# Taps of a depthwise convolution on ScalarE and GpSimd, and a bias product in bfloat16, in a three-layer block

## The reference

```python
def spatial_gating(u_a, v_a, ln_g, ln_b, w_s, b_s):
    u = jax.nn.gelu(u_a, approximate=False)
    v = layer_norm(jax.nn.gelu(v_a, approximate=False), ln_g, ln_b)
    v = v.reshape(bsz, seq // CHUNK, CHUNK, H_A, HD_A)
    w = w_s * jnp.tril(ones)[None]
    mixed = jnp.einsum('hts,bcshd->bcthd', w, v)
    mixed = mixed + jnp.transpose(b_s)[None, None, :, :, None]
    return u * mixed.reshape(bsz, seq, D_A)

def conformer_conv(val_b, gate_b, conv_w, conv_b, ln_g, ln_b):
    g = val_b * jax.nn.sigmoid(gate_b)
    c = depthwise causal convolution of g, 31 taps, + conv_b
    c = layer_norm over each of 4 groups of 128 channels
    return jax.nn.silu(c)
...
mix = jnp.concatenate([a_out, b_out], axis=-1)
x = x + jnp.einsum('bsc,cd->bsd', mix, w_out[l])
h = rms_norm(x, norm2_g[l])
f = jnp.square(jax.nn.relu(h @ w_ff1)); x = x + f @ w_ff2
```

## Time and profile before

| | us |
|---|---|
| median of 3 runs | 2577.37 (2575.87 to 2579.45) |
| profiled execution, its own time | 2576.84 |
| its span | 2575.0 |
| TensorE busy | 2354.4 (91%) |
| VectorE busy | 1537.0 (60%) |
| ScalarE busy | 963.0 (37%) |
| GpSimd busy | 206.9 (8%) |
| mean granted TensorE clock | 0.962 of full speed |

### The profile page before, as it was taken

The page is one execution under the profiler, slowest core; times in us unless marked ns, Lnnn a source line. Parts: engine busy times, 40 slices in busy tenths (PEclk is TensorE's granted clock), DMA queues, the critical chain, the costliest instruction groups (busy, mean ns, idle before and its releaser), DMA issues.

```text
span 2575.0 us, 30098 instructions
## 1 busy us (share of the span) xinstructions
PE 2354.4 (91%) x12784; PEld 1249.0 (49%) x12784; DVE 1537.0 (60%) x1970; ACT 963.0 (37%) x1367; POOL 206.9 (8%) x263
## 2 busy tenths in 40 slices
PE   6999649999999999898999877899999998888899
PEld 4445324444444444344444355664444445666764
DVE  5797766555444555576741388965534406888862
ACT  5244233312121222333221276752322215777741
POOL 0000002000000000432401101012000000000000
PEclk9997869999999999899999999999999998999999
DMA  4010000211111101003100000011130100000021
GB/s 173 33 66 33 33 0 2 97 66 49 50 40 59 66 33 66 33 3 131 66 33 33 33 1 1 1 69 63 66 131 33 67 1 33 1 1 1 1 82 50
DMA packets 50322, 116.00 MB, mean 45 GB/s; under 512 B 2384, under 2 KB 7817, under 8 KB 49804
## 3 DMA queue, kind: packets, MB, share of 16 engines
q1 hardware_dynamic: 48452, 105.39, 11.5%
q10 hardware_dynamic: 1736, 8.68, 0.8%
HBM read 101.49 MB, written 12.58 MB: 44 GB/s over the span
## 4 chain that ended last, share of the span: by engine, by line
PE 74%; DVE 15%; ACT 6%; issue 3%; POOL 1%; DMA 1%; ACTq 0%; DVEq 0%; POOLq 0%
PE PS L72 71%; DVE R L101 4%; PE PS L75 4%; ACT RG L81 3%; DVE R L93 2%; DVE RG L107 2%; DVE mx L110 2%; DVE RG L101 1%; ACT OV L84 1%; DVE scl L110 1%; DMA RG<-in_a_w_in 1%; DVE RG L93 1%; ACT R L81 1%; DVE oss L110 1%; ACT OV L81 0%
## 5 line engine op out<-in xcount | busy, mean ns | idle before, releaser
L72 PE MATMUL PS<-R,RG 128*128 128x512 f16 (+1 forms) x5472 | 1168.6, 375 | 10.1 <-DVE R L93 5.3
L72 PEld LDWEIGHTS PS<-R,RG 128*128 128x128 f16 (+1 forms) x5472 | 543.5, 103 | 631.1 <-issue 16.6
L72 PE MATMUL PS<-RG,R 128*128 128x512 f16 x2880 | 631.5, 379 | 4.1 <-DVE R L101 3.6
L72 PEld LDWEIGHTS PS<-RG,R 128*128 128x128 f16 x2880 | 281.9, 98 | 335.3 <-DVE R L101 4.1
L81 ACT ACTIVATE R<-PS,scl 128x512 f32<-128x512 f32 (+1 forms) x192 | 126.5, 686 | 712.5 <-PE PS L72 584.6
L72 PE MATMUL PS<-R,OV 128*128 128x64 f32 (+2 forms) x1456 | 196.8, 288 | 82.8 <-DVE R L101 50.6
L101 DVE SCALAR_TENSOR_TENSOR R<-PS,scl,R 128x512 f32<-128x512 f32 (+1 forms) x208 | 149.0, 746 | 164.2 <-PE PS L72 140.2
L107 DVE TENSOR_TENSOR_SCAN RG<-RG 128x127 f32<-128x127 f32 (+7 forms) x128 | 168.7, 1345 | 112.7 <-ACT RG L81 112.4
L72 PEld LDWEIGHTS PS<-R,OV 128*128 128x128 f32 x1456 | 181.5, 200 | 94.8 <-DVE R L101 52.2
L101 DVE SCALAR_TENSOR_TENSOR RG<-RG,scl 128x4096 f16<-128x4096 f32 (+1 forms) x43 | 188.7, 4388 | 50.3 <-ACT RG L81 50.3
L75 PE MATMUL PS<-ident,RG 128*128 128x128 f32 x864 | 150.5, 292 | 51.6 <-DVE RG L101 24.1
(11 more groups left out here) (113 smaller groups left out, 1546.4 us busy)
## 6 DMA issues: line engine op xcount, KB each, us to landing
RG<-in_w_ff SPq DMA_DIRECT2D x16, 2048.0 KB, 8.2
RG<-in_a_w_in SPq DMA_DIRECT2D x8, 2048.0 KB, 8.5
RG<-in_w_in SPq DMA_DIRECT2D x4, 2048.0 KB, 9.7
xspill<-R ACTq DMA_DIRECT2D x2, 4096.0 KB, 16.0
RG<-in_w_kv SPq DMA_DIRECT2D x4, 2048.0 KB, 8.6
RG<-in_b_w_in SPq DMA_DIRECT2D x4, 2048.0 KB, 8.1
R<-in_x SPq DMA_DIRECT2D x8, 512.0 KB, 9.1
RG<-in_w_out SPq DMA_DIRECT2D x2, 2048.0 KB, 7.7
```

The costliest lines, as they stand in the source:

```text
L72: return self.engine.matmul(*a, **k) if self.engine else Nothing()
```

## The change

- **Group 2 of the convolution.** Taps 0 to 20 become products on ScalarE: tap 0 straight into `MIX[:, 6]` with the bias, the others into one of three places (`MIX[:, 7]`, `MIX[:, 3]`, `MIX[:, 2]`), from where GpSimd adds them to `MIX[:, 6]`. From tap 16 on two places serve. VectorE does taps 21 to 30, which alternate with group 3's taps 1 to 10.
- **Bias of the gating.** `sgu_b` is loaded into three rows. VectorE makes three bfloat16 parts, one per row, whose sum is the float32 value; the product takes three rows of ones in bfloat16 (`identb`, which gets the identity only afterwards).
- **Gains of the attention.** `attention_gains` moves from ahead of V to behind the taps of t=1, and ScalarE's first V activation no longer waits for its end.
- **Last chain.** In `out_part(1)` blocks 0 to 2 of the first four units stand ahead of `centre(3)` and only block 3 behind `centre_spread(3)`; the second spread of chain 3 takes the bank of its first centring.
- **Order.** `centre(2)` stands behind unit 8 (was 12), its sums and spread at 11 and 14. The low half of tile 5 stands behind `gated_lows(0)`, that of tile 6 behind the second residual of part 1. `total(6)` and `convert(6)` move into chain 2; `total(7)` from ahead of part 1 into `up(0)`, and tile 7 is converted at uses 7 and 8 of tile 6 (was 5 and 6), tile 8 measured and converted one use later.

```diff
-for _j, _m, _c in ((7, None, (6, 5)), (8, (7, 1), (7, 2)), (9, (7, 6), (7, 7)), (10, (8, 6), (8, 8)),
+for _j, _m, _c in ((7, None, (6, 7)), (8, (7, 2), (7, 3)), (9, (7, 6), (7, 7)), (10, (8, 6), (8, 8)),
...
+        bias = R3[0:3, 1792:2304]
+        bias_part = OV[0:3, 1792:2048].bitcast(BF16)
+        bias_parts = OV[0:3, 1536:1792].bitcast(BF16)
...
+        pooled = 20
+        product_places = [MIX[:, 7, :], MIX[:, 3, :], MIX[:, 2, :]]
+        product_place = [None] + [i % 3 if i < 16 else i % 2 for i in range(1, pooled + 1)]
...
-                      + [(m, w) for m in (2, 3) for w in range(1, TAPS)])
+                      + [(m, w) for w in range(1, TAPS - pooled) for m, w in ((2, w + pooled), (3, w))]
+                      + [(3, w) for w in range(TAPS - pooled, TAPS)])
...
-                    e.matmul(b.rearrange("p (c t) -> p c t", c=4), ones[0:1, :],
-                             bsK[0:1, 128 * h:128 * h + 128]...broadcast_to([1, 4, P]),
+                    e.matmul(b.rearrange("p (c t) -> p c t", c=4), identb[0:3, :],
+                             bias_parts[:, 128 * h:128 * h + 128]...broadcast_to([3, 4, P]),
...
-            centre_spread(2)
+            for n, c, mi in out_order[:4]:
+                out_part(1, n, c, mi, range(3))
             centre(3)
             centre_sums(3)
             centre_spread(3)
...
-                out_part(1, n, c, mi)
+                out_part(1, n, c, mi, range(3, 4) if z < 4 else range(4))
...
+                    if m == 2 and w == pooled + 1:
+                        e.wait_ge(*sig("conv_pool").at(pooled))
...
+            for j in range(3):
+                e.tensor_copy(bias_part, bias).then_inc(*step.up())
+                e.wait_ge(*step.last())
+                if j == 0:
+                    e.tensor_scalar(bias_parts, bias_part, ident[0:3, 0:1], None, ALU.mult).then_inc(*step.up())
+                else:
+                    e.scalar_tensor_tensor(bias_parts, bias_part, ident[0:3, j:j + 1], bias_parts, ALU.mult,
+                                           ALU.add).then_inc(*step.up())
+                if j < 2:
+                    e.tensor_tensor(bias, bias, bias_part, ALU.subtract).then_inc(*step.up())
+                e.wait_ge(*step.last())
...
-                run_taps(0 if t == 3 else 3)
+                run_taps(4 if t == 0 else 0 if t == 3 else 3)
                 if t == 1:
                     factor(3)
+                    attention_gains()
...
-            run_taps(10)
+            run_taps(15)
             factor(5)
             run_taps(4)
-            convert_low(5)
-            run_taps(1)
...
-                    run_taps(1 if h < 3 else 0)
+                    run_taps(n if h < 2 else 0)
...
             gated_lows(0)
+            convert_low(5)
...
                 out_residual(0, n, c, mi)
-                run_taps(0 if z in (2, 4, 6, 8) else 1)
-                if z == 11:
-                    run_taps(max(0, 90 - taken[0]))
-            centre_factor(2)
-            run_taps(4)
-            mix_norm(2)
-            run_taps(6)
+                if z == 6:
+                    run_taps(max(0, 80 - taken[0]))
+                run_taps(0 if z in (2, 4, 6, 12, 14) else 1)
+            run_taps(2)
             mix_lows(2)
             run_taps(1000)
...
+            def products(*taps_):
+                e.wait_ge(*sig("glu").at(2, 1))
+                e.wait_ge(*full.at("xt", 0, 7))
+                for w in taps_:
+                    g, tap = G[:, 2, w:w + S], taps[:, 4 * w + 2:4 * w + 3]
+                    if w == 0:
+                        e.activation(MIX[:, 6, :], g, ACT.Identity, bias=gain("conv_b", 2), scale=tap)...
+                    else:
+                        same = [v for v in range(1, w) if product_place[v] == product_place[w]]
+                        if same:
+                            e.wait_ge(*sig("conv_pool").at(same[-1]))
+                        e.activation(product_places[product_place[w]], g, ACT.Copy, scale=tap)...
...
+                products(*((0, 1), (2,), (3, 4), (5, 6), (7, 8), (9,), (10,), (11, 12))[t])
...
+                if j < 4:
+                    products(13 + 2 * j, 14 + 2 * j)
...
+            def add_products(*taps_):
+                for w in taps_:
+                    e.wait_ge(*sig("tap_product").at(w))
+                    if w > 1:
+                        e.wait_ge(*sig("conv_pool").at(w - 1))
+                    e.tensor_tensor(MIX[:, 6, :], MIX[:, 6, :], product_places[product_place[w]],
+                                    ALU.add).then_inc(*sig("conv_pool").up(w))
...
+            for i in range(1, 4):
                 total(i)
+            add_products(*range(1, 10))
+            total(4)
+            add_products(*range(10, pooled + 1))
+            total(5)
```

More of the change, by code:

```diff
@@ L605, in centre_spread @@
                 for n in range(2):
-                    b = banks.take(("spread", "mix", n, mi))
+                    key = ("spread", "mix", n, mi)
+                    b = banks.take_at(key, banks.place[("cent", 3, 0)]) if (mi, n) == (3, 1) else banks.take(key)
                     e.wait_ge(*sig("diagonal").at("mix", n, mi))
@@ L610, in centre_spread, with out_part @@
                              start=True, stop=True).then_inc(*full.up("spread", "mix", n, mi))
-            def out_part(part, n, c, mi):
+            def out_part(part, n, c, mi, ks=range(4)):
                 key = ("out", part, n, c, mi)
                 i = 4 + c
[L616 to L619, removed]
+                if 0 in ks:
+                    b = banks.take(key)
+                    e.wait_ge(*sig("weight").at(i))
+                    e.wait_ge(*banks.free(key))
+                else:
+                    b = banks.ap(key)
+                for k in ks:
                     if part:
@@ L627, in out_part @@
                                       start=(k == 0 and ws + hs == 0), stop=(k == 3 and ws == 1))
-                mm.then_inc(*full.up(*key))
-                last_product[i] = key
+                if 3 in ks:
+                    mm.then_inc(*full.up(*key))
+                    last_product[i] = key
             centre(0)
@@ L1768, in total @@
                 out = R3[:, 0:2048].bitcast(F16) if i == 7 else w_slot(i)[:, 0:4096]
+                if i == 7:
+                    e.wait_ge(*full.at("out", 0, 1, 1, 3))
                 e.activation(out, w_raw(i), ACT.Abs, accum_out=w_col(i, 0)).then_inc(*sig("w_sum").up(i))
@@ L1842, in scalar, with products_done @@
             e.activation(lamt[:, 2:4], lamt[:, 0:2], ACT.Exp).then_inc(*sig("lambda_exp").up())
+            def products(*taps_):
[4 more added lines that the diff above has]
+                    if w == 0:
+                        e.activation(MIX[:, 6, :], g, ACT.Identity, bias=gain("conv_b", 2), scale=tap).then_inc(
+                            *sig("tap_product").up(0))
+                    else:
+                        same = [v for v in range(1, w) if product_place[v] == product_place[w]]
+                        if same:
+                            e.wait_ge(*sig("conv_pool").at(same[-1]))
+                        e.activation(product_places[product_place[w]], g, ACT.Copy, scale=tap).then_inc(
+                            *sig("tap_product").up(w))
+            def products_done(place):
+                e.wait_ge(*sig("conv_pool").at(max(v for v in range(1, pooled + 1) if product_place[v] == place)))
             for t in range(NT):
@@ L1928, in scalar @@
                 centre_root(mi)
+                if mi == 2:
+                    total(6)
                 mix_silu(mi)
                 mix_high(mi)
+                if mi == 2:
+                    convert(6)
             e.activation(col(127), epst[:, 0:1], ACT.Sqrt)
-            e.wait_ge(*full.at("out", 0, 1, 1, 3))
-            total(7)
             for z, (n, c, mi) in enumerate(out_order):
@@ L1964, in up @@
                         ff_relu(c, y)
+                    if c == 0 and z == 4:
+                        total(7)
             def split_f(c):
@@ L2278, in gpsimd @@
             measure(0)
-            for i in range(1, 6):
+            def add_products(*taps_):
[6 more added lines that the diff above has]
+            for i in range(1, 4):
                 total(i)
+            add_products(*range(1, 10))
+            total(4)
+            add_products(*range(10, pooled + 1))
+            total(5)
             e.wait_ge(*sig("gated_peak").at())
```

84 lines of the change are left out of this document (46 added, 38 removed).

## The result

The changed kernel took 2550.05 us (median of 4 runs, 2544.71 to 2560.25), the one before on the same chip 2576.9 (4 runs): a ratio of 0.9899, with a 95% interval of 0.9867 to 0.9931. That is 26.9 us less, where 27.3 were forecast. The profiled execution took 2548.93 us, with a span of 2546.9.

| us from the span's start | before | forecast | after |
|---|---|---|---|
| V normalised | 187.6 | 218.5 | 220.9 |
| VectorE reaches the gating | 212.7 | 243.9 | 245.9 |
| Q, last gating product | 240.3 | 251.5 | 253.1 |
| E, last tap | 354.3 | 331.0 | 334.2 |
| last chain, E to the first unit | 14.0 | 14.0 | 15.1 |

A forecast was written before the change was run, and what follows sets the result against it. TensorE is busy 91% of the span, so only its standstill (50.5 us, while VectorE runs taps) can give much back. 23.3 + 5.8 - 0.3 - 1.5 = 27.3 us less than 2577.37: 2550 us, range 2523 to 2564.

The forecast's parts named there:

- V normalised: VectorE, end of V's normalisation: forecast at 218.5 us from the span's start, with additions and two-input work in one queue.
- The hold: GpSimd additions and VectorE operations reading two SBUF tensors exclude each other: 2.0 us per addition, between 1.7 and 2.35.
- GpSimd's dry spell: GpSimd runs out of products after 12 additions, until about 196, as products 13 to 20 queue behind tile 4's conversion.
- Gating to Q: VectorE in the gating: eight products at about 0.65 us and two taps, 7.6 us, from 243.9 to 251.5.
- Q to E: From last gating product to last tap, sixteen output units and remaining taps: 79.5 us, ending at 331.0, 23.3 earlier.
- "slower" rival: Lower TensorE clock in the sixteen output units: 2.6 us more each, 41.5 in all, 2591 us; chance 0.05.
- After E: Behind the last tap: chain kept at 14.0 us, 27 matmuls done early save 5.8, tile 6's low half costs 0.3.
- Tile 7: Second up part: tile 7's weight ready at about 458.3, needed by TensorE at 456.9, on the old scale; 1.5 us lost.
- Bias: Gating: bfloat16 bias products shorten TensorE's work by 11 us, costed at nothing because VectorE arrives later.
- gains: Attention gains moved behind tap group t=1, so taps fill VectorE's 7.24 us idle wait for the exponential of lambda.
- without exclusion: Rival: GpSimd additions do not hold VectorE's taps; Q at about 227, E at 306.5, 2525 us; chance 0.15.
- The hand-over: Rival: products 13 to 20 and additions wait for each other's few places; 29.6 us instead of 21.4, 2558 us; chance 0.12.

The follow-up runs named there:

- without the early blocks: Changed kernel with blocks 0 to 2 of the first four output units put back behind chain 3's spread: 2553.86 us, ratio to before 0.9914.
- The block within the chain: Changed kernel with block 2 of the first four output units moved into chain 3, only blocks 0 and 1 ahead: 2554.42 us, ratio to before 0.9929.
- The kernel with late additions: Against the changed kernel, a bundle: group 2's taps all on VectorE, group 3's last 12 added on GpSimd during the output units: 2531.08 us, ratio to before 0.9839.

## Why the prediction was right

The mechanism held at each step: longer VectorE operations and no gap ahead of the gating, then less left over behind it. The errors are of size. Up to the second up part they add to 5.4 us: V 2.4 late, V to Q 0.8 short, Q to E 1.6 long, E to the first sums 2.5 long, the rest 0.3 short. The whole time hides them, because the 6.2 us further on, in the stretch where only the granted clock differs, went the other way. That was luck.

- **The hold.** Forecast 2.0 us, bounds 1.7 and 2.35. Over the 19 additions that met such an operation it was 38.1 us, 2.01 each. The share read from the products of before was right for additions, another operation on the same shape. By the Trainium skill, SBUF — State Buffer, section "SBUF: two separate sides", the second instruction is blocked for the whole of the first, which would make it 2.35; the measured hold is 2.01, and the measurement decides.
- **V normalised: 2.4 late.** The holds are one fewer than I counted (1.9 less). But I gave the statistics 2.7 us where eight of 0.81 (151.82 to 152.63) are 6.5, and left out the 1.65 that VectorE waits for ScalarE's high half of tile 3. These leave the sum within 1.1 of what was measured.
- **GpSimd's dry spell.** Forecast until about 196 after twelve additions; it was 171 to 185 after nine. The factor of tile 4 began at 180.7 and not at 184.6, because the three additions missing there stood behind `total(4)`. It costs nothing in sum, since the queue of both engines is as long in either order.
- **Gating to Q.** Reached 24.9 us after V (25.4 forecast), through in 7.26 (7.6). TensorE's 11.17 ahead of its last unit comes by way of ScalarE from VectorE's factor of tile 5; VectorE itself never waited.
- **Q to E: 81.1 against 79.5.** The step that was mis-sized is the first output unit. I took 2.6 us from the earlier trace rows; it ran at the lower level and took 5.28. Only this unit did (the next 36 matmuls took 7.93), so of the "slower" rival one unit of the eleven that it needed came true.
- **After E.** Here the size was furthest off: 3.0 won where 5.8 - 0.3 were forecast. The 27 matmuls are 5.8 us, as shown without the early blocks. But I kept the last chain's 14.0 us and it took 15.1, and the units behind it took 19.99 instead of 18.3. The block within the chain shows that the 1.7 goes with an empty chain; what sets the 1.1 is open.
- **Tile 7.** Its stall was 1.06 where I had 1.5. The kernel with late additions converts it one use earlier and has none.
- **Bias** at nothing and **gains** as idle time filled: both shown.
- **Sums.** Two steps of the working do not add up to the last digit: 136.7 with its four terms is 184.4 and not 184.6, and 458.3 - 456.9 is 1.4 and not 1.5.

The rivals: without exclusion the time would have been 2523 to 2526, as worked out (2525), but the exclusion is there. The hand-over sets no pace. Of the sixteen output units only the first ran at the lower level. What the prediction did not ask is whether the tap transfer is worth its price. Its own numbers held the answer: 20 x 2.0 of hold against 26.4 to 27.2 of taps saved. I had both terms in one sum and never set them beside each other.

What stays open: the rest of the program scattered by 22 us over the profiled executions of all these kernels, in unchanged code. The traces say where (mostly one stretch of some 120 us) and as what (longer matmuls at a lower granted clock); no experiment says what sets it. Nor has any kernel the old order of the taps, or the late additions alone.

## What to carry to other kernels

Before work goes to GpSimd, price the hold and not GpSimd's own time: here an addition cost VectorE 2.0 us and saved a tap of 1.3, so it could only pay where the hold falls on a wait of VectorE. Split a bundled change and read each part at an anchor just behind it; this gain came from waits of VectorE that went, by one moved step and the order of its taps, and none of it from the part that the change is named after. When matmuls are done early to shorten the work behind a dependent chain, leave some of them in the chain: here that was worth 1.7 us.

## What was not expected of the hardware

- A GpSimd operation over the same tile that only writes (two fills, 1.96 us) left VectorE's taps at 1.21 us; one that also reads (an addition, 2.35 alone) held VectorE for 2.0 us.
- Additions and the eight normalisations of 0.67 alternate: five additions were let in over eight back-to-back instructions, 15.57 us in all, of which the first five took 2.5 to 2.9 us each. VectorE's unbroken stream did not keep GpSimd out.
- With twelve matmuls of 512 columns in the chain, six on either side of the sums, its granted clock was 0.80 and not 0.58, and behind it 1.00 and not 0.91: 84 matmuls took 18.30 us (two kernels) and not 19.99 (seven kernels).
- In one stretch of unchanged code the same 834 matmuls took between 97.6 and 117.6 us in different executions, at granted clocks of 0.91 to 0.76, with the other engines as busy as ever.
